# Products that nobody reads, on TensorE while it waits, in a transformer block with experts followed by two retrieval layers

## The reference

```
h = rms_norm(x, norm_attn); proj = h @ w_in            # [256,1024] @ [1024,7712]
... attention, gates ...
x = x + merged @ w_out
h2 = rms_norm(x, norm_ffn)
logits = h2 @ w_router                                  # pick a group, then two experts of it
y = 0
for e in range(32):                                     # only the chosen tokens are computed
    he = silu(h2 @ w_gate[e]) * (h2 @ w_up[e])
    y = y + combine[:, e] * (he @ w_down[e])
x = x + y
... second block: xn = rmsnorm(x, norm_mix); h = x + mixer(xn); h = h + peer(...); twice
```

## Time and profile before

| what | value |
|---|---|
| time, median of 3 executions | 2231.38 us (2229.43 to 2231.91) |
| the profiled execution's own time | 2230.41 us |
| its span, first to last instruction | 2228.6 us |
| TensorE busy | 1831.3 us, 82% |
| VectorE busy | 1307.7 us, 59% |
| mean granted TensorE clock | 0.943 of full |
| mean DMA rate | 345 GB/s |

### The profile page before, as it was taken

How to read it: one execution, slowest core, us unless ns; L and a number is a source line. 1 busy time by engine, 2 the same in 40 slices (tenths; PEclk the granted TensorE clock), 3 DMA queues, 4 the chain that set the end, 5 groups by cost and what they waited for, 6 DMA issues and landing times.

```text
span 2228.6 us, 18733 instructions
## 1 busy us (share of the span) xinstructions
PE 1831.3 (82%) x5744; PEld 875.8 (39%) x5744; DVE 1307.7 (59%) x3325; ACT 484.9 (22%) x1214; POOL 672.5 (30%) x593
## 2 busy tenths in 40 slices
PE   8999996988779969888768877768888777878875
PEld 4445554332234635344223323324343433434332
DVE  1343424111123356767777978897677798777764
ACT  1232321111101222222221212222121222222221
POOL 1110001110000024434444434444333445444442
PEclk9999996999989989999999988889999988999999
DMA  6432237999773199999999999999999999999995
GB/s 239 167 118 104 102 130 315 413 417 418 304 291 137 54 381 371 422 420 421 421 421 422 384 422 419 421 421 421 413 421 421 384 422 414 420 422 421 421 420 243
DMA packets 112295, 768.82 MB, mean 345 GB/s; under 512 B 15856, under 2 KB 16544, under 8 KB 20416
## 3 DMA queue, kind: packets, MB, share of 16 engines
q0 software_dynamic: 78928, 542.37, 59.2%
q1 hardware_dynamic: 30672, 215.17, 24.3%
q10 hardware_dynamic: 2592, 10.04, 1.2%
HBM read 769.62 MB, written 10.49 MB: 350 GB/s over the span
## 4 chain that ended last, share of the span: by engine, by line
DMA 31%; DVE 17%; PE 10%; issue 10%; POOL 4%; ACT 1%; POOLq 0%; DVEq 0%; ACTq 0%
DMA arena<-in_c_rows_dram,arena 31%; DVE arena L2509 7%; POOL arena L2577 4%; PE banks L308 4%; PE banks L2169 2%; DVE x L2519 2%; PE banks L2495 1%; PE banks L1796 1%; DVE arena L2440 1%; DVE arena L2402 1%; DVE arena L2405 1%; PE banks L339 1%; DVE arena L2444 1%; PE banks L354 1%; DVE arena L2411 1%
## 5 line engine op out<-in xcount | busy, mean ns | idle before, releaser
L2495 PE MATMUL banks<-arena 128*128 128x512 f32 x1792 | 891.4, 644 | 274.7 <-ACT arena L2559 269.7
L2577 POOL DMA_INDIRECT arena<-in_c_rows_dram,arena x512 | 594.2, 1161 | 819.1 <-PE banks L2495 540.2
L2509 DVE CUSTOM_DVE_ANT_0 arena<-arena,xn 128x1024 f32<-128x1024 f32 x512 | 624.6, 1222 | 261.3 <-DMA arena<-in_c_rows_dram,arena 259.9
L2495 PEld LDWEIGHTS banks<-arena 128*128 128x128 f32 x1792 | 349.7, 204 | 762.7 <-ACT arena L2559 370.5
L308 PE MATMUL banks<-ring,hT 128*128 128x512 f32 (+1 forms) x672 | 284.3, 579 | 0.0
L2559 ACT ACTIVATE arena<-ident,small 128x128 f32<-128x128 f32 x448 | 158.8, 395 | 542.5 <-DVE small L2516 525.3
L308 PEld LDWEIGHTS banks<-ring,hT 128*128 128x128 f32 x672 | 123.5, 190 | 141.1 <-issue 139.0
L360 ACT COPY arena<-banks 128x512 f32<-128x512 f32 (+4 forms) x211 | 97.2, 488 | 323.5 <-PE banks L354 125.1
L2550 ACT ACTIVATE small<-small 128x2 f32<-128x2 f32 x256 | 52.2, 204 | 493.7 <-DVE small L2509 493.6
L386 POOL TENSOR_TENSOR small<-small 128x1 f32<-128x1 f32 (+4 forms) x24 | 34.2, 1423 | 360.7 <-DVE small L382 358.8
L365 DVE COPY arena<-banks 128x512 f32<-128x512 f32 (+1 forms) x45 | 30.5, 680 | 134.1 <-PE banks L1332 71.9
(11 more groups left out here) (297 smaller groups left out, 1592.4 us busy)
## 6 DMA issues: line engine op xcount, KB each, us to landing
arena<-in_c_experts_dram SPq DMA_DIRECT2D x53, 1024.0 KB, 27.1
ring<-in_c_experts_dram SPq DMA_DIRECT2D x33, 1024.0 KB, 27.5
ring<-in_c_w_in_dram SPq DMA_DIRECT2D x30, 1024.0 KB, 4.8
ring<-in_c_odd_w_in_dram SPq DMA_DIRECT2D x21, 1024.0 KB, 9.4
ring<-in_c_w_q_dram SPq DMA_DIRECT2D x20, 1024.0 KB, 9.1
ring<-in_c_even_w_in_dram SPq DMA_DIRECT2D x14, 1024.0 KB, 5.5
arena<-in_c_rows_dram,arena POOLq DMA_INDIRECT x512, 13.8
ring<-in_c_odd_w_out_dram SPq DMA_DIRECT2D x8, 1024.0 KB, 9.7
```

The lines of the kernel that those rows point to most:

```text
L2495: r = e.matmul(banks[:, bank_of[("acc", L, c, hf)], :], diag[:, diag_of[m], :], rows[:, m % NB, D + hf * 512:D + (hf + 1) * 512], start=fi ...
L2509: e.tensor_tensor_reduce(u, u, xn[:, c, :], 1.0, 0.0, ALU.mult, ALU.add, hid3[:, c, h, k:k + 1]).then_inc(ve.sem, ve.up(("u", p)))
L2577: e.indirect_dma_start(rows[:, b, :], None, table_uv, bass.IndirectOffsetOnAxis(ap=eix[:, c, 16 * h + k:16 * h + k + 1], axis=0)).then_inc ...
```

## The change

A helper makes n products of 128x512 columns into the next bank and signals TensorE's semaphore. Nobody reads that bank. TensorE calls it five times: 5 products at the start on zeroed columns of hT, 3 after the table "tab", 8 directly after the expert tiles, 8 when the experts' results are stored (both semaphores `ys_out`), and 3 when chunk 0 of x has its sum. `pe.mark("moe")` stays where it was in the list, behind the experts' part, and so the last 19 products now stand ahead of it.

```diff
+        def pe_idle_work(e, name, n, cols):
+
+            b, before = rings.take(("idle", name))
+            if before is not None:
+                e.wait_ge(*emptied[before])
+            for _ in range(n):
+                r = e.matmul(banks[:, b, :], cols[:, 0:P], cols, start=True, stop=True)
+            r.then_inc(pe.sem, pe.up(("idle", name)))
+            emptied[("idle", name)] = (pe.sem, pe.n)
...
         def tensor_first(e):
+            e.wait_ge(ve.sem, ve.at("zeros"))
+            pe_idle_work(e, "start", 5, hT[:, 0:2, :].rearrange("p k t -> p (k t)"))
             e.wait_ge(fetched("ident").sem, fetched("ident").at("all"))
...
         def vector_first(e):
+            e.memset(hT[:, 0:2, :], 0.0).then_inc(ve.sem, ve.up("zeros"))
...
             r.then_inc(pe.sem, pe.up("table"))
+            e.wait_ge(ve.sem, ve.at("tab"))
+            pe_idle_work(e, "tokens", 3, x[:, 0, 0:512])
             pe_tiles(e, 0, NTILE, xg_in)
...
+        steady = gain[:, gain_of["ffn"], 0:512]
+
         def tensor(e):
             tensor_first(e)
             tensor_moe(e)
+            pe_idle_work(e, "last rows", 8, steady)
+            for i in range(2):
+                e.wait_ge(ys_out[i].sem, ys_out[i].at("all"))
+            pe_idle_work(e, "results", 8, steady)
+            e.wait_ge(ve.sem, ve.at(("x", "mix0", 0)))
+            pe_idle_work(e, "norm", 3, steady)
             pe.mark("moe")
             tensor_even(e)
```

## The result

| kernel | time, median | spread | executions |
|---|---|---|---|
| before | 2231.94 us | 2229.43 to 2236.09, and one of 2314.47 | 20 |
| changed | 2234.95 us | 2230.40 to 2239.40 | 20 |

The ratio is 1.0015, with a 95% interval of 1.0008 to 1.0021: about 3 us slower, and between 1.8 and 4.7 by the interval. One execution of before ran in a slow state, at 2314.47 us, and stands outside the comparison. The forecast was 2231.7, a sum of +0.3 us, which is no change that can be told, in a range of 2228.9 to 2235.0. The median lies at the very edge of that range, and a loss clear of the spread was not foreseen.

What follows compares the result with a forecast made beforehand. TensorE's waits followed by work at the lower clock were taken as the bound, with the experts bound by their weights. Start -2.3, tokens -0.2 and results +2.8 sum to +0.3 us: median 2231.7, range 2228.9 to 2235.0.

Steps and rivals of the forecast that it cites:

- Gain 2.3 us: Start: chunk 0's eight records take 3.4 us in place of 5.74, bounds 0 and 2.3.
- if the level holds: Start: condition that the upper clock lasts over the gap after the five products, under 2 us to 9.82.
- what is won at 12.59 should arrive at the experts: Start to experts: TensorE has no long wait from 20 to 345 us, so the start's gain carries through.
- The Trainium skill's rule on transposes: Start: transposes don't count as busy for the full clock; by it the gap is 4.3 us and the gain 0.
- The row at 385.7: First expert tile: clock 1.00 after sixteen transposes and 0.35 us of products, so transposes count as work; start gains 2.3.
- Gain 0.2 us: Tokens: only the first pair of L1313 records leaves the lower level, bounds 0 and 1.6.
- That buys almost nothing: Tokens: transposes take about 2.1 us, not 3.68, but L1313 waits for a DVE copy ending about 385.2.
- The moved wait: Results: ACT's square also waits for the norm's three products, starting 3.2 us later; loss 2.8, between 1.2 and 3.2.
- the eight records: Results: chunk 0's records after the transposes take 5.46 us as before, with the clock's rise inside.
- The start doesn't lift or doesn't hold the level: Rival, start: no gain there, sum +2.6, 2234.0 us; chance 0.22.
- ACT free: Rival, results: ACT does not wait, clock stays up, gain 2.0 there, total -4.5, 2226.9 us; chance 0.06.

Runs made afterwards that it cites:

- experiment 12: The changed kernel run once more without any edit: 2235.40 us against 2232.21 for the kernel before, ratio 1.0015.
- experiment 10: Kernel before with only the start's zeroing and five products, plus two 128x448 products between chunk 0's transposes and first weight product: 2231.45 against 2231.76 us, ratio 0.9996.
- experiment 7: Kernel before with only the calls at the results, six products instead of three in the last, mark still behind them: 2238.09 against 2232.21 us, ratio 1.0025.
- experiment 5: Changed kernel with the mark "moe" ahead of the last three calls and without the three products after the table: 2228.45 against before's 2231.76 us, ratio 0.9984.
- experiment 2: Kernel before with only the last three calls (8, 8 and 3 products), mark behind them: 2236.22 against 2232.51 us, ratio 1.0013.
- experiment 8: Kernel before with only the calls at the results, and the mark moved ahead of them: 2229.09 against 2232.21 us, ratio 0.9986.

## Why the prediction was wrong

- **Start: the step "Gain 2.3 us", the largest miss.** The price was right for an execution in which the level holds (18.33 to 15.96 in experiment 12's profile), but it was entered in full, with "if the level holds" and with the sentence that what is won at 12.59 should arrive at the experts. Both failed. Without the two more products of experiment 10 the level held up to the first products with weights in three of five profiles. And where it held, the clock fell near 31 us in four of five. What is left at 340 us is about 0.8 us, and the start alone measures -0.5 with an interval that includes 0. The sentence rested on TensorE's lack of waits; that excludes a new wait, and not a slower clock.
- **The Trainium skill's rule on transposes** ("TensorE: Matmul & The Clock Gate", section "Part 4: PE-mode transpose"). The row at 385.7 was taken against it, and the traces bear that out: in experiment 7's profile TensorE makes nothing but 16 transposes between 375.5 and 384.9, and the granted clock rises at 385.0, with the first expert product. By the rule the start's level should never have held, as the prediction worked it out; it held in three of five profiles. So the rule does not explain the part that failed. In the three that kept it, 3.3 to 3.7 us lay between the last added product and L339, in the two that lost it 4.0 and 4.1. The block ended earlier in these because its clock had risen earlier.
- **Tokens: the step "Gain 0.2 us", with a lower bound of 0.** "That buys almost nothing" was right for the reason given: the DVE copy decides, and L1326 came no earlier for the fast transposes. I did not ask what faster transposes leave behind: a gap of 2.49 us where 0.42 had been. Before, the slow transposes lasted nearly until the product could start, and the clock rose right behind them, at 385.7. In three of four profiles SP's next fetch is 1.5 us late for it. That a loss reaches the time is not shown: alone the three products measure +1.4 us with an interval from -0.7 to +3.4, and taking them out in experiment 5 gained nothing.
- **Results: the mechanism right, the size perhaps too small.** The moved wait, the square 3.2 us late, the full idle gap and the fall of the clock all came as written. The term was put at 2.8 us between 1.2 and 3.2; the calls alone measure 3.7, from 0.9 to 4.9, and in the three profiles chunk 1's transposes come 4.3, 4.0 and 3.3 us later after x. The excess in the two profiles of the changed kernel is the eight records, which I let run as before, with the rise 3.9 us after their start: they took 6.59 and 6.31 us and not 5.46. In experiment 2's profile they took 5.62, and the lateness of the square is nearly all.
- **The sum.** Forecast -2.3 - 0.2 + 2.8 = +0.3. Measured place by place: -0.5 + 1.4 + 3.7 = +4.6, against +3.0 for the whole, which the intervals allow. The profiles of the first and last place give -0.8 and +3.3 to +4.3. Of the 2.7 us between +0.3 and +3.0 the start's term alone accounts for 1.5 to 1.8. All three terms erred about the level of the clock behind the added products.
- **The rivals.** "The start doesn't lift or doesn't hold the level", at 2234.0, was nearest to the measured 2234.95. That is in part luck: the start did lift the clock, and held it in most executions profiled, and the sum has a small gain and no loss for the tokens. "ACT free" was refuted in the changed kernel and tried in experiment 8; with the mark ahead the times give 3.1 us at the results, and the profiles 2.0 (11.62 to 9.62), which is what I had worked out for it.

What stays open is why the clock falls near 31 us and near 601 us in some executions and not in others, and with that how the gains of the start and the tokens come out in a typical one.

## What to carry to other kernels

Work added to an idle engine is free only if nobody counts it: look up every wait on that engine's semaphore, and marks in the instruction list above all. Products that hold a clock must reach up to the work that they are meant for. Here a block that ended 2 to 4 us earlier left the real work at the lower level in most executions, and a speed-up of what lay between opened just that gap. If a chain behind another engine decides when the next product starts, faster transposes ahead of it are worth nothing, and they can cost something where the longer ones kept TensorE at work until that product. And a gain in an early stretch is worth what is left of it further on: read it there, at a place that nothing has changed, before it is entered in a sum.

## What the runs showed of the hardware

The moment at which the clock changes is not tied to the program. The same kernel showed the fall at the start (0.50 in 12.8 to 16.1) in one execution and none in another. Products on zeros do lift the clock: the 10 records on zeroed columns took 6.77 us in one profile and 7.43 in the other, and not the 8.5 of ten at the lower level. Transposes lift it too. In experiment 7 TensorE did nothing from 375.5 to 380.7, made 16 transposes, and was at the upper level with the first record behind them:

```profile
375.50:380.70 5.20, 0.00 (x0) 0.00 (x0) 4.56 (x36) 0.00 (x0) 3.17 (x3) 0.50 0.83 311
380.70:384.70 4.00, 3.68 (x16) 3.28 (x16) 2.07 (x14) 2.65 (x11) 0.98 (x1) 0.50 0.13 36
385.00:385.20 0.20, 0.20 (x2) 0.18 (x4) 0.20 (x1) 0.20 (x1) 0.00 (x0) 1.00 0.21 21
```

And a stretch in which TensorE is busy throughout can still lose the upper level: 27 to 31 us in experiment 10 has 4.00 of 4.00 us busy, 34 records with most of them narrow, and the clock was at 0.50 from 31.0 on. The same four us with the same 34 records in experiment 5 were followed by 1.00.
